# Encoder block on one core: first pass from unnormalised, host-transposed tokens, RMS factor applied when the heads leave PSUM

## The reference, cut to what matters

```python
def rms_norm(x, g):
    y = xf * lax.rsqrt(jnp.mean(xf * xf, axis=-1, keepdims=True) + EPS)
    return y * g

mod = silu(c) @ w_ada + b_ada
sh_a, sc_a, gt_a, sh_m, sc_m, gt_m = split(mod, 6)
h = rms_norm(x, g_pre_attn) * (1.0 + sc_a) + sh_a
proj = h @ w_in            # 4160 columns: q_a, k_a, v_a, q_b, ckv, k_pe
...
```

## Time and profile before

| what | before |
|---|---|
| median of 3 runs | 2012.2 us (2012.09 to 2014.27) |
| the profiled execution, its own time | 2012.37 us |
| its span, first to last instruction | 2010.3 us |
| TensorE busy | 1981.6 us, 99% |
| VectorE busy | 1720.5 us, 86% |
| ScalarE busy | 1006.0 us, 50% |
| moved by DMA | 433.31 MB |

### The profile page before, as it was taken

How to read it: one execution, slowest core, us unless ns; L and a number is a source line. 1 busy time by engine, 2 the same in 40 slices (tenths; PEclk the granted TensorE clock), 3 DMA queues, 4 the chain that set the end, 5 groups by cost and what they waited for, 6 DMA issues and landing times.

```text
span 2010.3 us, 30608 instructions
## 1 busy us (share of the span) xinstructions
PE 1981.6 (99%) x11131; PEld 1736.3 (86%) x11131; DVE 1720.5 (86%) x2053; ACT 1006.0 (50%) x1425; POOL 160.1 (8%) x173
## 2 busy tenths in 40 slices
PE   7999999999999999999999999999999999999998
PEld 6887888878888878999999999998888888888886
DVE  7987988787877788999999999988898898898866
ACT  6464223698732374565656565655343343333322
POOL 0000000257400000000000000000300000000000
PEclk8999999999999999999999999999999999999999
DMA  9988778500477745667676766668746546556542
GB/s 354 372 294 310 238 221 255 186 1 22 147 263 261 240 156 190 214 210 234 210 232 210 231 210 231 212 210 337 249 179 251 202 174 250 190 185 251 178 178 84
DMA packets 260467, 433.31 MB, mean 216 GB/s; under 512 B 27680, under 2 KB 155296, under 8 KB 247456
## 3 DMA queue, kind: packets, MB, share of 16 engines
q1 hardware_dynamic: 242576, 361.42, 53.0%
q0 software_dynamic: 15936, 63.97, 8.7%
q10 hardware_dynamic: 1872, 6.82, 0.9%
HBM read 367.68 MB, written 64.49 MB: 215 GB/s over the span
## 4 chain that ended last, share of the span: by engine, by line
PE 91%; DVE 5%; ACT 3%; issue 1%; DMA 0%; POOL 0%; SPq 0%; ACTq 0%; POOLq 0%; DVEq 0%
PE bank L2800 9%; PE bank L2801 9%; PE bank L2802 9%; PE bank L2822 9%; PE bank L2824 9%; PE bank L2823 9%; PE bank L2331 6%; PE bank L2333 6%; PE bank L2332 6%; PE bank L2883 1%; PE bank L2882 1%; PE bank L2881 1%; PE bank L2344 1%; PE bank L2346 1%; PE bank L2345 1%
## 5 line engine op out<-in xcount | busy, mean ns | idle before, releaser
L1377 ACT ACTIVATE hi<-w 128x1024 fp32r<-128x1024 f32 x168 | 178.4, 1062 | 264.8 <-PE bank L2824 197.5
L2822 PE MATMUL bank<-hi,y_use 128*128 128x512 f32 x784 | 306.6, 391 | 0.0
L2823 PE MATMUL bank<-lo,y_use 128*128 128x512 f32 x784 | 305.1, 389 | 0.0
L2824 PE MATMUL bank<-hi,y_use 128*128 128x512 f32 x784 | 305.1, 389 | 0.0
L1296 ACT ACTIVATE hi<-a 128x1024 fp32r<-128x1024 f32 x196 | 206.6, 1054 | 154.4 <-DVE a L2038 141.8
L2035 DVE TENSOR_TENSOR lo<-a,hi 128x1024 fp32r<-128x1024 f32 x196 | 239.3, 1221 | 43.5 <-ACT hi L1296 43.1
L2800 PE MATMUL bank<-h_hi,hi 128*128 128x256 f32 x896 | 253.7, 283 | 0.9 <-DVE c_b L2065 0.9
L2801 PE MATMUL bank<-h_lo,hi 128*128 128x256 f32 x896 | 253.6, 283 | 0.0
L2802 PE MATMUL bank<-h_hi,lo 128*128 128x256 f32 x896 | 253.6, 283 | 0.0
L822 ACT ACTIVATE hi<-raw 128x1024 fp32r<-128x1024 f32 (+2 forms) x120 | 120.5, 1007 | 229.4 <-PE bank L2333 85.2
L2150 DVE TENSOR_TENSOR lo<-w,hi 128x1024 fp32r<-128x1024 f32 x168 | 204.7, 1226 | 32.0 <-ACT hi L1377 31.0
(11 more groups left out here) (400 smaller groups left out, 4693.1 us busy)
## 6 DMA issues: line engine op xcount, KB each, us to landing
w<-in_w_mlp_out SPq DMA_DIRECT2D x128, 512.0 KB, 4.8
a<-in_w_mlp_in SPq DMA_DIRECT2D x112, 512.0 KB, 4.5
y_use<-y_dram SPq DMA_DIRECT2D x53, 1024.0 KB, 9.3
y_dram<-y_out POOLq DMA_DIRECT2D x28, 1792.0 KB, 6.8
w_turned<-in_w_ada_t SPq DMA_DIRECT2D x32, 1024.0 KB, 7.3
raw<-in_w_mod SPq DMA_DIRECT2D x64, 512.0 KB, 4.9
raw<-in_w_ada SPq DMA_DIRECT2D x36, 512.0 KB, 4.8
raw<-in_w_out SPq DMA_DIRECT2D x32, 512.0 KB, 4.7
```

The lines of the kernel that those rows point to most:

```text
L1377: nc.scalar.activation(hi[w.slot()][:], weight(np, i, h)[:], ACT.Copy).then_inc(hi_ready, 1)
L2822: mm(bank[b + m][:], yh, hi[s][:, q, :], start=j == 0, stop=False)
L2823: mm(bank[b + m][:], yh, lo[s][:, q, :], start=False, stop=False)
L2824: ins = mm(bank[b + m][:], yl, hi[s][:, q, :], start=False, stop=j == PAIRS - 1)
```

## The change

The host adds one input, `x_t`, the tokens transposed (channels by tokens). The first 16 chunks take their 128 by 512 block of it (`x_raw`, 256 KB, ring of 4) instead of the turned and normalised `x_t` tile; only the channel gain is applied. `x_tok` is loaded later, one tile behind the weights of chunks 1, 3, 5 and 8, squared (whole tile on ScalarE) in ScalarE's steps 1, 4, 7 and 10, scaled on ScalarE one step later, and turned by TensorE in groups of four transposes between the heads of two chunks each (3 and 4, 6 and 7, 9 and 10, 12 and 13, behind heads 2 and 5), all in bank 7, each group waiting for ScalarE's copy of the group before. The inverse RMS is spread over the partitions behind chunk 14 (four transposes, `spread_r`), copied to `r_spread`, and the heads are moved out by VectorE with one multiplication by it (`head_out`). Ten transposes of the identity follow the spreading of silu. The ring of `w_turned` is 3 instead of 4. Cut to its core:

```diff
-X_BANKS = 4
-X_BANK = (7, 4, 5, 6)
+WARM = 10
+W_RING = 3
+X_AFTER = (1, 3, 5, 8)
+X_SQUARE = (1, 4, 7, 10)
+X_TURN = (3, 6, 9, 12)
...
             def load_mod(n):
 
-                if n >= RING:
-                    sp.wait_ge(col_summed, n - RING + 1)
...
+                if n >= W_RING:
+                    sp.wait_ge(col_summed, n - W_RING + 1)
...
+            def load_x_raw(k):
+
+                if k >= RING:
+                    sp.wait_ge(h_made, 2 * (k - RING + 1))
+                sp.dma_start(x_raw[k % RING][:], x_raw_d[k]).then_inc(raw_landed[k % RING], 16)
...
-            for t in range(NT - 1):
-                load_x(t)
-            load_mod(0)
-            load_x(NT - 1)
-            load_weights(0)
-            for n in range(1, CHUNKS):
+            for n in range(CHUNKS):
                 load_mod(n)
+                if n < KD:
+                    load_x_raw(n)
                 load_weights(n)
+                if n in X_AFTER:
+                    load_x(X_AFTER.index(n))
...
+            def x_scale(t):
+
+                act.wait_ge(x_inverse, t + 1)
+                nc.scalar.activation(x_tok[t][:], x_tok[t][:], ACT.Copy, scale=rstd[:, t, 0:1]).then_inc(x_normed, 1)
+
+            def x_copy(t, kk):
+
+                act.wait_ge(x_turned, NT * t + kk + 1)
+                src = bank[7][:].rearrange("p (k n) -> p k n", k=4)
+                nc.scalar.activation(x_t[:, KD - 4 * kk - 4:KD - 4 * kk, t * P:(t + 1) * P], src, ACT.Copy).then_inc(x_t_ready, 1)
...
-                        nc.scalar.activation(dst, x_at(k), ACT.Copy, scale=g).then_inc(h_made, 1)
+                        nc.scalar.activation(dst, x_raw[k % RING][:], ACT.Copy, scale=g).then_inc(h_made, 1)
...
+            for n in range(CHUNKS):
                 start_w_hi(n)
                 start_h(n)
+                if n in X_SQUARE:
+                    x_square(X_SQUARE.index(n))
+                if n - 1 in X_SQUARE:
+                    x_scale(X_SQUARE.index(n - 1))
+                for m in range(2):
+                    if n - 1 - m in X_TURN:
+                        for kk in range(2 * m, 2 * m + 2):
+                            x_copy(X_TURN.index(n - 1 - m), kk)
                 if n == KD:
-                    for i in range(4):
-                        head_copy(i, q_park[:, i, :])
...
+                    act.wait_ge(spread, 5)
+                    nc.scalar.activation(r_spread[:], bank[7][:], ACT.Copy).then_inc(spread_copied, 1)
...
+                stt(dst, bank[i][:], SCALE_B, r_spread[:], ALU.mult, ALU.mult).then_inc(heads_out, 1)
...
+                if n == KD + 1:
+                    dve.wait_ge(spread_copied, 5)
+                    for i in range(4):
+                        head_out(i, q_park[:, i, :])
+                    dve.wait_ge(h_made, 2 * (KD + 1))
+                    head_out(4, q_o[:, HEADS + EARLY[4], :])
+                if n == KD + 3:
+                    dve.wait_ge(h_made, 2 * (KD + 3))
+                    for i in (5, 6):
+                        head_out(i, q_o[:, HEADS + EARLY[i], :])
...
+            def turn_between(k, i):
+
+                for m in range(2):
+                    if k - m in X_TURN and i in (2, 5):
+                        turn_x(X_TURN.index(k - m), 2 * m + (i == 5))
```

More of the change, by code:

```diff
@@ L205, in build @@
         lo = [sb(f"lo{i}", 36 + 4 * i, [QROWS, COLS], F32R) for i in range(RING)]
-        x_tok = [sb(f"x_tok{t}", at, [D]) for t, at in enumerate((76, 92, 100, 108))]
-        x_junk = sb("x_junk", 68, [D])
+        x_tok = [sb(f"x_tok{t}", at, [D]) for t, at in enumerate((100, 108, 76, 172))]
+        x_junk = [sb(f"x_junk{t}", at, [D]) for t, at in enumerate((68, 68, 68, 108))]
+        x_raw = [sb(f"x_raw{i}", 188 + 2 * i, [T]) for i in range(RING)]
+        r_spread = sb("r_spread", 204, [T])
         h_hi, h_lo = sb("h_hi", 52, [KD, T], F32R), sb("h_lo", 84, [KD, T], F32R)
@@ L236, in build @@
         x_res = sb("x_res", 148, [NT, D])
-        w_turned = [sb(f"w_turned{i}", at, [D]) for i, at in enumerate((148, 156, 164, 172))]
+        w_turned = [sb(f"w_turned{i}", at, [D]) for i, at in enumerate((148, 156, 164))]
         silu_b = sb("silu_b", 180, [D])
@@ L315, in build @@
         y_put = y_dram.rearrange("g k p j n -> g j p k n")
+        x_raw_d = a["x_t"].rearrange("(k p) t -> k p t", p=P)
         x_d = a["x"].rearrange("b (t p) d -> (b t) p d", p=P)
@@ L327, in build @@
         raw_landed = [sem(f"raw_landed{i}") for i in range(PROJ_RING)]
-        w_turned_landed = [sem(f"w_turned_landed{i}") for i in range(RING)]
+        w_turned_landed = [sem(f"w_turned_landed{i}") for i in range(W_RING)]
         raw_used, hi_ready, w_used = sems("raw_used hi_ready w_used")
@@ L781, in build @@
         landed_at = {}
-        twice = [proj_raw(PROJ_BLOCKS, j) for j in range(UNITS_D)] + [KV_RAW + 2 * j for j in range(KV_UNITS)]
+        twice = [*range(KD)] + [proj_raw(PROJ_BLOCKS, j) for j in range(UNITS_D)] + [KV_RAW + 2 * j for j in range(KV_UNITS)]
         for r in range(OUT_RAW):
@@ L845, in x_square @@
                     act.wait_ge(x_sq, t)
[L846 to L856, removed]
+                if t == NT - 1:
+                    act.wait_ge(x_t_ready, 2 * NT)
+                nc.scalar.activation(x_junk[t][:], x_tok[t][:], ACT.Square, accum_out=stat[:, t, 0:1]).then_inc(x_sq, 1)
+                act.wait_ge(x_sq, t + 1)
+                nc.scalar.activation(stat_s[:, t, 0:1], stat[:, t, 0:1], ACT.Sqrt, scale=1.0 / D, bias=eps[:]).then_inc(x_sqrt, 1)
+            def x_scale(t):
[5 more added lines that the diff above has]
+                nc.scalar.activation(x_t[:, KD - 4 * kk - 4:KD - 4 * kk, t * P:(t + 1) * P], src, ACT.Copy).then_inc(x_t_ready, 1)
             def start_w_hi(n):
@@ L1553, in _ @@
                     h_low(n - 1)
+                if n - 1 in X_SQUARE:
+                    x_invert(X_SQUARE.index(n - 1))
                 column_out(n)
@@ L2413, in head_chunk @@
                         ins.then_inc(heads_done, 1)
+                    turn_between(k, i)
                 ins.then_inc(w_used, 1)
+                if k == KD - 2:
+                    spread_r()
             def rotary_chunk(k):
+                if k == 0:
+                    pe.wait_ge(spread_copied, 5)
                 both, _ = weight_cols(KD + k, KPE)
@@ L2441, in latent_chunk @@
                 return ins
-            for t in range(NT):
-                if t:
-                    pe.wait_ge(x_normed, t + 1)
-                turn_x(t)
             first_heads()
```

123 lines of the change are left out of this document (45 added, 78 removed).

## The result

| what | before | after |
|---|---|---|
| median of 16 runs | 2012.09 us (2010.87 to 2014.27) | 2016.38 us (2014.65 to 2018.61) |
| ratio, 95% interval | | 1.0022 (1.0015 to 1.0029) |
| the profiled execution, its own time and span | 2012.37, 2010.3 us | 2016.85, 2015.1 us |
| first matmul of the heads | 27.48 | 11.77 |
| chunk 16's first matmul | 105.37 | 104.67 |

The changed kernel is 4.3 us slower, about 0.2%. That is within the range of the prediction and 2.6 us over its point. It is 0.3 us beyond the 4 us that the prediction took as its line between "same" (chance 0.62) and "slower" (0.22). TensorE starts 15.7 us earlier, 0.7 us of that is left at chunk 16, 5.9 us are lost in the next 75 us, and 0.4 come back behind them.

What follows compares the result with a forecast made beforehand. TensorE, busy 99% of the span, was taken as the bound. Chunk 16 0.9 us earlier and evictions +2.5 gave +1.6 on the profiled execution, so 2013.8 us for the median; range 2007.5 to 2019.

Steps and rivals of the forecast that it cites:

- The start: First head matmul at 11.6 instead of 27.48 us, -15.9, worked out from bytes, 420 GB/s and VectorE's step.
- From chunk 3 to chunk 16: From TensorE's release at 36.4: rest of chunk 3, 12 chunks, 15 transpose groups, loop and clock; chunk 16 at 104.5 us.
- The clock: TensorE's granted clock falls behind chunk 3's 3.9 us wait: +1.4 us, bounds 0 and 3.4.
- The evictions: Seven head evictions on VectorE make chunk 17 late by 1.5 us and chunk 19 by 1.0: +2.5, bounds 0 and 4.8.
- The loads: DMA rate taken as 420 GB/s for the new start, which asks for 17% more bytes per chunk.
- the slower rival: Full DMA engines move only 352 GB/s, M(4) and M(9) land late: +6.9 us, 2020.7; loads or ring bind, chance 0.20.
- loads bind: Early chunks wait for landings at 352 GB/s: +6.9 us, 2020.7; chance 0.20 together with the ring of three.
- late places hide each other: No clock fall (-1.4) and evictions finding VectorE ahead (-2.5): 2009.9 us, or 2008.7 with chunk 3's copy in time; chance 0.16.
- The step that failed: Near chunk 31's end: the later copy of `silu_second` stands in ScalarE's idle time, costed at nothing.
- edits costed at nothing: Root's table load, identity transposes, later copy of `silu_second` and ring of three for M: no cost in the sum.
- if anything behind chunk 31 changes its length by over 1 us: Sign that the prediction is wrong: everything behind chunk 31 was to keep its length within 1 us.
- The table load and the transposes of the identity: Ahead of the first head matmul: table load hidden behind silu's spreading, ten transposes in TensorE's idle time before 11.6; no cost.

Runs made afterwards that it cites:

- e9: Changed kernel with both repairs (e6), without the ten transposes of the identity: 2011.1 us, 0.9996 of the kernel before.
- e6: Changed kernel with eight ScalarE issues behind the first projection block's second `hi`, heads moved out by ScalarE and multiplied by r_spread on VectorE behind h_low(31): 2010.98 us.
- e2: Changed kernel with the seven heads moved out by ScalarE as before, multiplied by r_spread on VectorE behind h_low(31): 2015.04 us.
- e4: Changed kernel with both repairs (e1, e2), token tiles loaded behind chunks 1, 5, 6, 9, squared in 1, 6, 7, 10, turned from 4, 7, 9, 12: 2011.34 us.
- e7: e4 with tiles loaded behind chunks 3, 5, 6, 9, squared in 4, 6, 7, 10, turned from 5, 7, 9, 12, ScalarE's copies ahead of scaling and squares: 2017.38 us.
- e5: Kernel before, with only ScalarE's copy of `silu_second` moved from behind h(30) to behind h(31): 2015.56 us, 1.0015 of before.
- e1: Changed kernel with ScalarE's eight load and store issues moved from ahead of `tmp` to behind the second `hi` of the first projection block: 2013.8 us.
- e8: Changed kernel without the ten transposes of the identity ahead of the first matmul: 2016.1 us, 1.0021 of the kernel before.
- e10: Repeat of e6, the changed kernel with the two repairs alone, run beside e9: 2011.36 us, 0.9996 of the kernel before.
- e3: Changed kernel with the first token tile turned one chunk later, in chunks 4 and 5 instead of 3 and 4: 2017.32 us, 1.0029 of the kernel before.

## Why the prediction was right, and where it was not

**The start, right.** First head matmul at 11.77 (forecast 11.6), M(4)'s column at 29.67 (29.3 for its landing), the copy starts at 35.77 and TensorE is released at 36.49 (36.4), its wait is 3.45 (3.9). The 15.9 us of earlier start was the largest term of the sum, and it came out of bytes, a rate and one step of VectorE.

**From chunk 3 to chunk 16, right in sum.** 36.49 to 104.67 is 68.2 us; the terms (1.2 + 57.4 + 7.8 + 0.3 + 1.4) give 68.1. Two of them missed and cancel: the 15 groups of transposes cost 0.45 to 0.58 each, 7.0 in all (forecast 7.8), and short lags behind `h_lo` add up to 1.0 (forecast 0.3). Chunk 16 begins 0.7 earlier than before, forecast 0.9; that the two agree so closely is in part luck, since profiles of the same program part by 1.4 us at this place. The clock fell behind the wait of chunk 3 to 0.57 over 4 us, the same number as the stretch it was taken from, and the group and six matmuls behind the wait took 3.25 us where the later pace gives 1.8: 1.4 lost, as forecast. This too differs between executions: 0.50 in e9 and 1.00 in e6 over the same 4 us.

**The evictions, right.** Waits of 1.49 and 0.73 us at chunks 17 and 19, forecast 1.5 and 1.0; +2.44 to the end of chunk 31, forecast +2.5. e2 takes the whole of it away by moving them back.

**The loads, right by the measured rate.** 412 to 415 GB/s from 5 to 80 us in the change, where the forecast took 420 and the slower rival 352. No `column` from 60 us on waits for a landing. The Trainium skill (DMA: Bandwidth & Descriptors, Specifications) puts the limit of HBM for a core at about 358 GB/s; the run disagrees with this over 75 us, on a chip with one core at work, and agrees with the fabric ceiling of 435 in the same table. The rivals *loads bind* and *late places hide each other* both fell. At the full rate, though, landings still set the early chunks: in e4 VectorE waits 2.90 and 2.71 us for M(6) and M(7), in e7 2.06 to 2.72 for M(5) to M(7), and TensorE waits behind it at chunks 4 to 6. Neither of these two orders of the tokens brought a gain. An order with only two tiles ahead of M(7) would need another place for what the squares write, and wasn't tried.

**The step that failed** is, among the edits costed at nothing, "The later copy of `silu_second` stands in ScalarE's idle time before the last chunk's end." The copy does stand there. What was not counted is what is queued behind it: eight issues, 5.1 us of ScalarE's queue with a cover of only 0.88 us before `tmp`, and a low clock behind the longer wait. It cost 1.81 + 1.63 = +3.4 us in the change, 3.3 us in e5, where nothing else was changed, and went away in e1. With 3.4 in the sum the forecast would have been 2017.2, 0.8 over the measured median. So the time lay within the range although a term of 3.4 was missing: the range reached to 2019 for the sake of the loads, which did not bind, and its upper side caught a cost that it was not made for. That is luck. The sum had named the work that hides the copy, and not what it costs when that cover ends, which was the question to ask. The sentence that would have shown it wrong was there, "if anything behind chunk 31 changes its length by over 1 us", and it did, by 1.81 and 1.63.

The table load and the transposes of the identity cost nothing, as said; e8 shows the second, the first only by the start at 11.77.

## What to carry to other kernels

When an instruction moves down its engine's queue, follow the queue to the next thing that somebody waits for, and count DMA issues on a compute engine as work of that engine: the instructions behind them wait for the issues, not for their data. A load that starts nothing urgent belongs behind the next instruction on the path, not ahead of it. When the work before the main stretch is moved into it, the early start is worth only what is left once that work is done in its new place and the inputs have landed: here, of 15.7 us, about 7.6 come back as 17 groups of transposes, 3.5 as the wait in chunk 3, and 2.8 as a slower chunk 0 (6.46 us, before 5.10) and the low clock behind that wait, and 0.7 is left. With both side costs repaired (e6, e9, e10) the change ends 0.3 to 1.1 us under the kernel before, with an interval that includes no difference.

## What the runs showed that was not expected

- A wait of 1.9 us more cost 3.3, but not in every profile. Behind the gap at the first projection unit (from one matmul's start to the next) 24 matmuls took 7.00 to 7.22 us in the change, e2, e5 and e8, whose gaps were 2.86, 2.55, 2.92 and 2.58, with a granted clock of 0.66 to 0.76 over 170 to 175 us. In e3, with a gap of 2.64, they took 5.59 at 1.00, as they did (5.57 to 5.62) behind gaps of 1.04 to 1.06 in before, e1, e4, e6, e7, e9 and e10. Behind the 3.8 us gap in chunk 3 the same kernel's clock differed: 1.00 over 36 to 40 us in e6, 0.60 in e10. e4, whose gaps between 20 and 50 us were all 2.03 or shorter, had 1.00 there.
- The granted clock of a stretch does not always give the pace. In e8 it reads 1.00 over 12 to 16 us, yet the first seven matmuls behind an idle time of 4.27 us take 3.12 us (11.76 to 14.88), 0.45 each, where 0.228 is the pace at full clock; in the change, with 0.57 in the same stretch, they take 2.77 us (11.77 to 14.54), and in e4, with 1.00 like e8, 1.69 (11.48 to 13.17).
- The DMA engines held 412 to 415 GB/s for 75 us with rows of 2 KB among the transfers, while before the same engines at a share of 0.98 moved 345 at 90 to 100 us.
